# All attention of a two-block transformer kernel taken in pairs of score tiles, with transposes in place of diagonal products

## The chip, the cores and the metric

The kernel runs on one core of one Trainium2 chip. Its engines are called here PE (TensorE, matrix products), DVE (VectorE), ACT (ScalarE), POOL (GpSimd) and SP (SyncE, which issues most of the transfers). The metric is the time of one execution on the device in microseconds (us), lower is better; the median of several executions is given. All data are fp32, and every product with a weight is made from a high and a low part of both operands (three products of the fp32r type in place of one), so PE has three times the work of a plain product. The products inside the attention are plain fp32 products; in the trace each of them is two PE records ("passes").

## The reference, cut to what matters

Two blocks run one after the other on 256 tokens of width 1024. The first one has a layer with retention and a layer with neighbourhood attention ("nat", 16 heads of width 64, 256 image tokens against 256 image keys and 256 context keys), the second one has two layers with three attention branches each.

```python
# nat_mixer: s_nb are scores with a bias by position, s_cx those against the context
p = jax.nn.softmax(jnp.concatenate([s_nb.reshape(B, H, GRID_W, nk), s_cx], axis=-1), axis=-1)
o = einsum(p_nb, vw) + einsum(p[..., nk:], vc)
# _diff_attention, 4 heads, two score tiles each
w = probs(q1, k1) - lam * probs(q2, k2)
o = jnp.einsum('bhqk,bkhd->bqhd', w, v)
# _moba_attention (4 heads of 128; one block of 256 keys, so plain causal attention with a bias)
# _dense_causal_attention, "mla" (8 heads, q and k of width 96, v of width 64)
p = jax.nn.softmax(jnp.where(rel >= 0, s, NEG_INF_2), axis=-1)
o = jnp.einsum('bhqk,bkhd->bqhd', p, v)
```

## The kernel before, in words

Each engine has its own program, written in the same order of stages, and they meet by semaphores. A weight product is a `gemm`: groups of 256 weight columns, a group being two or four chunks (a chunk fills one of the four PSUM banks `bank`), each chunk 24 passes of PE for a depth of 1024. The weights of a group arrive by DMA in `raw`; ACT makes `w_high` and DVE `w_low` of them one or two groups ahead. A chunk is taken out of PSUM by ACT and DVE in turn.

Attention is cut into tiles of 128 queries of one head, and a tile into units: one unit is one softmax (nat, moba and mla have one unit in a tile, diff two, of which the second is multiplied by minus lambda). There are 32 nat units of 512 keys, and in each of the two layers of the second block 16 diff units, 8 moba units and 16 mla units, half of 128 keys and half of 256. One unit goes this way:

- PE `scores`: the product of q and k into `aux[0]` or `aux[1]` (L1948) and the bias added by a second product with a constant matrix (L1949). For nat and diff the product has 64 rows, heads lying at partitions 0 to 63 or 64 to 127.
- DVE `row_max`: the largest score of a row (L1455), and its sign turned (L1456).
- ACT `exponentials`: exp with the row sum beside it (L1016).
- DVE `diagonal`: the reciprocal of the sum (L1465) and the identity times it, a diagonal matrix `dg` (L1468, L1471 with lambda).
- PE `turn`: the probabilities times the diagonal, per 128 keys (L1965), which transposes and divides them in one product, into `aux[2]`; the two units of a diff tile are summed here.
- ACT `turn_out`: `aux[2]` copied to SBUF (L997).
- PE `values`: the turned probabilities with v, per 128 keys, into `aux[3]` (L1979). For nat and mla the result fills 64 partitions, `128*64` in the trace.
- ACT `out_high` (L1005) and DVE `out_low` (L1480): high and low part of the result. There is one bank `aux[3]`, so `values` of a tile waits for `out_low` of the tile before.

The generator `attention` on each engine yields after each unit, and `alongside` puts groups of other weight products between the units: for nat in four calls (nat0 to nat3) of eight units, beside the three products q, k and v of the next four heads, one whole group after units 3, 6 and 8, and none beside nat3; for diff and mla by a rule on the number of units (`narrow`), with DVE and ACT one group behind PE; moba runs bare but for its first units. Four heads' bias tables for nat are fetched by POOL into `tt`, which holds two heads, and DVE adds a mask to them with six instructions a head (L1491).

Of the kernel before, what the change touches and what calls it, by code (L numbers as in the profile page):

```python
# [14 lines left out]
F32 = mybir.dt.float32  # L15
F32R = mybir.dt.float32r
I32 = mybir.dt.int32
ALU = mybir.AluOpType
# [3 lines left out]
P = 128  # L22
# [84 lines left out]
def program(nc, A):  # L107
    ctx = ExitStack()
    with ctx:
# [44 lines left out]
        def scope(tensors):  # L154
            with ExitStack() as s:
# [18 lines left out]
        att_bufs = [("pexp", [P, 2, 512], F32), ("ptr", [P, 2, 512], F32), ("dg", [P, 2, P], F32),  # L174
                    ("stat", [P, 4, 8], F32)]
        ptr = hf
        nah, nal, nq, nk, nv, tt, pexp, dg, stat = scope(first_named(first[:5], "n_") + [
            ("nat_high", [P, DC, T], F32R), ("nat_low", [P, DC, T], F32R), ("nq", [P, DC, T], F32),
            ("nk", [P, DC, T2], F32), ("nv", [P, 4, D], F32), ("tt", [P, 2, 6, 64], F32), att_bufs[0]] + att_bufs[2:])[5:]
        (yh, yl, yt, sq2, hf2, ah, al, sig, v2, v3, mq, mk, mv, t5, ang, oraw,  # L180
         pexp2, dg2, stat2) = scope([
# [5 lines left out]
             ("oraw", [P, 4, T], F32), ("pexp2", [P, 4, T], F32), ("dg2", [P, 4, P], F32),  # L187
             ("stat2", [P, 4, 8], F32)])
        ptr2 = hf2
# [269 lines left out]
        unit_total = tile_total = 0  # L459

        def add_att(name, tiles, bufs):
            nonlocal unit_total, tile_total
            a = Att()
            a.name, a.tiles, a.bufs = name, tiles, bufs
            a.u0, a.t0 = unit_total, tile_total
            a.units = [(t, i) for t, tile in enumerate(tiles) for i in range(len(tile["units"]))]
            unit_total += len(a.units)
            tile_total += len(tiles)
            a.u1, a.t1 = unit_total, tile_total
            a.narrow = name[:3] != "nat"  # L470
            a.slots = 4 if a.narrow else 2
            a.lead = 2 if a.narrow else 1
            atts[name] = a

        tiles = []
        for hd in range(NH):
            c, r = hd // 2, 64 * (hd % 2)
            for qt in range(2):
                tiles.append(dict(
                    units=[dict(qk=(nq[r:r + 64, c, P * qt:P * qt + P], nk[r:r + 64, c, :]), coef=None,  # L480
                                bias=(0, T, tt[:, hd % 2, 2 - 2 * qt:6 - 2 * qt, :]))],
                    keys=512, rows=(r, r + 64),
                    v=lambda k, hd=hd: nv[:, k, 64 * hd:64 * hd + 64],
                    out=(nah[r:r + 64, c, P * qt:P * qt + P], nal[r:r + 64, c, P * qt:P * qt + P]),
                    head=hd))
# [1786 lines left out]
```

## Time and profile before

| | |
|---|---|
| Median of 3 runs | 3334.35 us (3333.47 to 3337.49) |
| The profiled execution | 3335.01 us |
| Its span in the trace | 3333.2 us |
| PE busy | 3189.2 us, 96% of the span |
| PE weight loads busy | 2758.7 us, 83% |
| DVE busy | 1838.9 us, 55% |
| ACT busy | 1167.0 us, 35% |
| Mean granted PE clock | 0.976 of full |

The execution is about 1.8 us longer than the span, which is what lies around the traced program. The busy time of an engine is the union of its records. A record of PE reaches from the start of a pass to the modelled end of it, about 0.17 us after the next may begin, so that what a pass costs is read from the start of one to the start of the next, not from its duration. "Idle <- X" names what released the engine; "issue" stands where the profile found no releaser.

### The profile page before, as it was taken

Reading aid. Unit: us, or ns where it says so; the run is one execution under the profiler, and the core shown is the slowest. Engines: PE = TensorE matmul, PEld = TensorE weight load, DVE = VectorE, ACT = ScalarE, POOL = GpSimd, SP = SyncE. Lnnn points to the kernel's source line nnn. Section 1 sums busy time; section 2 is a strip of 40 time slices with the busy share of each in tenths; the row PEclk is TensorE's granted clock in tenths of the full one; section 3 lists DMA queues with packets and bytes.
Section 4 is the critical chain, followed back from the end, with each engine's and each line's share of the span. In section 5 each row is a group of like instructions: output and inputs, shape, how many; then the busy total and the mean of one; then the engine's idle time right before and its main releaser. Section 6 shows DMA issues by size and latency. Waiting matters only on the chain. (4 is left out here: it accounts for less than half of the span.)

```text
span 3333.2 us, 47025 instructions
## 1 busy us (share of the span) xinstructions
PE 3189.2 (96%) x19173; PEld 2758.7 (83%) x19173; DVE 1838.9 (55%) x3647; ACT 1167.0 (35%) x2007; POOL 62.3 (2%) x106
## 2 busy tenths in 40 slices
PE   7999999999989999999998999999989999999898
PEld 4788887888868888788887777999878999788898
DVE  1677654444458876533324434556556655655665
ACT  2322223233232222332223324444444444344443
POOL 1000000000000000000000000000001000001000
PEclk9999999999989999899998999999999999999999
DMA  8445542212226565433323222655225454324452
GB/s 263 114 137 170 150 161 64 66 61 83 70 64 180 191 191 176 133 90 106 94 82 94 63 63 69 195 168 187 77 89 177 152 183 133 114 89 140 139 189 90
DMA packets 501214, 421.36 MB, mean 126 GB/s; under 512 B 9946, under 2 KB 497674, under 8 KB 501000
## 3 DMA queue, kind: packets, MB, share of 16 engines
q1 hardware_dynamic: 497976, 412.33, 40.3%
q0 software_dynamic: 3024, 6.03, 0.7%
q8 instruction: 152, 2.49, 0.3%
q14 instruction: 62, 0.51, 0.0%
HBM read 417.20 MB, written 1.12 MB: 126 GB/s over the span
## 5 line engine op out<-in xcount | busy, mean ns | idle before, releaser
L1254 DVE TENSOR_TENSOR w_low<-raw,w_high 128x1024 fp32r<-128x1024 f32 (+2 forms) x720 | 761.9, 1100 | 358.5 <-ACT w_high L839 357.4
L839 ACT ACTIVATE w_high<-raw 128x1024 fp32r<-128x1024 f32 (+2 forms) x720 | 647.8, 948 | 689.3 <-PE gemm L1872 408.9
L1872 PE MATMUL gemm<-xh,w_high 128*128 128x512 f32 (+1 forms) x1792 | 675.9, 377 | 22.3 <-DVE xl L1290 22.3
L1872 PE MATMUL gemm<-xl,w_high 128*128 128x512 f32 (+1 forms) x1792 | 666.3, 372 | 0.0
L1872 PE MATMUL gemm<-xh,w_low 128*128 128x512 f32 (+1 forms) x1792 | 666.0, 372 | 0.0
L1872 PEld LDWEIGHTS gemm<-xh,w_high 128*128 128x128 f32 x1792 | 341.2, 190 | 94.2 <-issue 18.3
L1872 PEld LDWEIGHTS gemm<-xh,w_low 128*128 128x128 f32 x1792 | 341.3, 190 | 63.2
L1872 PEld LDWEIGHTS gemm<-xl,w_high 128*128 128x128 f32 x1792 | 341.9, 191 | 60.7 <-issue 0.7
L1872 PE MATMUL gemm<-yh,w_high 128*128 128x256 f32 x1216 | 353.6, 291 | 15.4 <-DVE yl L1315 7.1
L1872 PE MATMUL gemm<-yl,w_high 128*128 128x256 f32 x1216 | 348.1, 286 | 0.0
L1872 PE MATMUL gemm<-yh,w_low 128*128 128x256 f32 x1216 | 347.7, 286 | 0.0
L1225 DVE SCALAR_TENSOR_TENSOR macc<-raw,sc,macc 128x256 f32<-128x256 f32 x728 | 302.1, 481 | 4.0
L1872 PE MATMUL gemm<-hid_high,w_high 128*128 128x512 f32 (+1 forms) x704 | 262.3, 373 | 0.0
L1872 PE MATMUL gemm<-act_high,w_high 128*128 128x256 f32 (+1 forms) x880 | 251.1, 285 | 8.6 <-DVE yt L1422 8.6
L1872 PE MATMUL gemm<-hid_high,w_low 128*128 128x512 f32 (+1 forms) x704 | 259.3, 368 | 0.0
L1872 PE MATMUL gemm<-hid_low,w_high 128*128 128x512 f32 (+1 forms) x704 | 259.2, 368 | 0.0
L1872 PEld LDWEIGHTS gemm<-yh,w_high 128*128 128x128 f32 x1216 | 235.5, 194 | 20.6 <-issue 17.4
L1872 PE MATMUL gemm<-act_low,w_high 128*128 128x256 f32 (+1 forms) x880 | 248.5, 282 | 0.0
L1872 PE MATMUL gemm<-act_high,w_low 128*128 128x256 f32 (+1 forms) x880 | 248.3, 282 | 0.0
L1872 PEld LDWEIGHTS gemm<-yl,w_high 128*128 128x128 f32 x1216 | 235.9, 194 | 0.1
L1872 PEld LDWEIGHTS gemm<-yh,w_low 128*128 128x128 f32 x1216 | 235.4, 194 | 0.0
L1398 DVE TENSOR_TENSOR hf<-sq,gemm 128x512 f32<-128x512 f32 (+1 forms) x88 | 54.6, 621 | 283.5 <-PE gemm L1872 283.5
(307 smaller groups left out, 4429.2 us busy)
## 6 DMA issues: line engine op xcount, KB each, us to landing
raw<-in_ffn_w_in SPq DMA_DIRECT2D x176, 512.0 KB, 5.2
raw<-in_w_mod SPq DMA_DIRECT2D x72, 1024.0 KB, 7.0
raw<-in_w_in SPq DMA_DIRECT2D x50, 1024.0 KB, 5.3
raw<-in_w_up SPq DMA_DIRECT2D x32, 1024.0 KB, 5.5
raw<-in_w_down SPq DMA_DIRECT2D x32, 1024.0 KB, 5.2
raw<-in_ffn_w_out SPq DMA_DIRECT2D x32, 768.0 KB, 4.5
raw<-in_ret_w_in SPq DMA_DIRECT2D x24, 1024.0 KB, 5.2
raw<-in_ffn_w_out SPq DMA_DIRECT2D x32, 640.0 KB, 4.1
```

The costliest lines, as they stand in the source:

```text
L839: act.activation(wh[i % SPL][:, a:b], raw[slot_of["w", i]][:, a:b], ACT.Copy).then_inc(w_high, 1)
L1225: dve.scalar_tensor_tensor(out=acc, in0=raw[slot][:, WB * k:WB * k + WB], scalar=sc[:, k, v:v + 1], in1=acc, op0=ALU.mult, op1=ALU.add).th ...
L1254: dve.tensor_tensor(wl[slot][:, a:b], raw[slot][:, a:b], wh[i % SPL][:, a:b].bitcast(F32), ALU.subtract).then_inc(w_low, 1)
L1398: dve.tensor_tensor(hf[:, pr % 2, 0:tok], sa[:, pr % 2, 0:tok], ps[:, 0:tok], ALU.mult).then_inc(odd_free, 1)
L1872: ins = pe.matmul(out, l_, r_, start=first and j == 0, stop=last and j == 2)
```

## The change

Units are now taken in pairs. For nat and mla a pair is two neighbouring heads with the same 128 queries, for moba two heads, for diff the two softmaxes of one tile. For a pair:

- `scores` makes the two products with 64 rows one directly behind the other (nat and diff: into `aux[0]` and `aux[1]`), then the two biases. For moba and mla both units share a bank, and two pairs can be open at once; for nat and diff the next pair's products wait until both exponentials are out.
- `row_max` has the sign in the same instruction (`negate=True`), and for moba and mla one instruction serves both units.
- `divide` takes the place of `diagonal`: one reciprocal for both sums, and the probabilities themselves are multiplied in SBUF (for diff scaled and added, so that one tile is left).
- `turn` is a transpose on PE (`pe.transpose`) of the divided probabilities, four for each of the 32 nat units, and 24 for each of diff, moba and mla over both layers (48 for mla).
- `values` writes the two heads of a nat or mla pair alternately into the lower and upper 64 partitions of `aux[3]`, and `out_high` and `out_low` take both at once.
- There is one nat attention of 16 pairs, and the nine products nat_q1 to nat_v3 run beside it by single chunks (24 chunks, one after nearly every half pair), until three pairs before its end.
- `tt` holds four heads, and the mask is one instruction a head.

The core of the diff:

```diff
+                def divide(p):
+                    g, t = a.p0 + p, a.pairs[p]
+                    dve.wait_ge(p_ready, 2 * g + 2)
+                    chain(dve.reciprocal(stat_of(a, p, 2), stat_of(a, p, 1)))
+                    first_, second = probs_of(a, p, 0), probs_of(a, p, 1)
+                    if a.kind == "dif":
+                        co = t["layer"]
+                        chain(dve.tensor_scalar(second, second, stat_of(a, p, 2, 1), lamn[:, co:co + 1], ALU.mult, ALU.mult))
+                        dve.scalar_tensor_tensor(out=first_, in0=first_, scalar=stat_of(a, p, 2, 0), in1=second,
+                                                 op0=ALU.mult, op1=ALU.add).then_inc(p_scaled, 2)
+                    else:
+                        dve.tensor_scalar(first_, first_, stat_of(a, p, 2, 0), None, ALU.mult).then_inc(p_scaled, 1)
+                        dve.tensor_scalar(second, second, stat_of(a, p, 2, 1), None, ALU.mult).then_inc(p_scaled, 1)
...
-                        for kt in range(tile["keys"] // P):
-                            for q in range(nu):
-                                uq = u - nu + 1 + q
-                                ins = pe.matmul(aux[2][:, P * kt:P * kt + P], pe_[:, uq % a.slots, P * kt:P * kt + P],
-                                                dg_[:, uq % a.slots, :], start=q == 0, stop=q == nu - 1)
+                    if a.nat:
+                        pe.wait_ge(p_scaled, 2 * g + i + 1)
+                        if g or i:
+                            pe.wait_ge(pt_out, 2 * g + i)
+                        for kt in range(4):
+                            ins = pe.transpose(aux[2][:, P * kt:P * kt + P], probs_of(a, p, i)[:, P * kt:P * kt + P], ident)
...
+                scores(0)
                 yield 1
-                for j, (t, i) in enumerate(a.units):
-                    nu = len(a.tiles[t]["units"])
-                    if j + a.lead < n:
-                        scores(j + a.lead)
-                    turn(j)
-                    if i == nu - 1 and t >= 1:
-                        values(t - 1)
+                for p in range(n):
+                    if p + 1 < n:
+                        scores(p + 1)
+                    if p:
+                        values(p - 1)
+                    turn(p, 0)
                     yield 1
-                values(len(a.tiles) - 1)
+                    turn(p, 1)
+                    yield 1
+                values(n - 1)
```

Place one, PE in the nat attention: one unit as the kernel before has it between two others (L1948 is the product, L1949 the bias, L1965 the turn, L1979 the values).

```order
L1948 MATMUL aux<-nk,nq 128x512
L1949 MATMUL aux<-tt,cst 128x256
L1965 MATMUL aux<-dg,pexp 128x128 x4
L1979 MATMUL aux<-hf,nv 64x128 x4
L1872 MATMUL gemm<-xh,w_high 128x256
L1872 MATMUL gemm<-xl,w_high 128x256
L1872 MATMUL gemm<-xh,w_low 128x256
```

The same place of the changed kernel, one half of a pair's round (L1960 the two products, L1964 the two biases, L2013 the values of the pair before, L1985 the transposes of the first unit, then a chunk of a weight product).

```order
L1960 MATMUL aux<-nk,nq 128x512 x2
L1964 MATMUL aux<-tt,cst 128x256 x2
L2013 MATMUL aux<-xt,nv 64x128 x8
L1985 MATMUL aux<-cst,pexp 128x128 x4
L1881 MATMUL gemm<-w_high,xh 128x256
L1881 MATMUL gemm<-w_low,xh 128x256
L1881 MATMUL gemm<-w_high,xl 128x256
```

Two products, two biases and eight values now stand together, and the values come ahead of the turn. The other half of the round is four transposes and a chunk.

Place two, PE in the mla attention of the first layer, kernel before: two units between two groups of weight products.

```order
L1948 MATMUL aux<-mk,mq 128x128
L1949 MATMUL aux<-cst 128x128
L1965 MATMUL aux<-dg,pexp 128x128
L1979 MATMUL aux<-hf,mv 64x128 x2
L1948 MATMUL aux<-mk,mq 128x256
L1949 MATMUL aux<-cst 128x128
L1965 MATMUL aux<-dg,pexp 128x128 x2
L1979 MATMUL aux<-hf,mv 64x128
```

The same place of the changed kernel:

```order
L1960 MATMUL aux<-mk,mq 128x128
L1964 MATMUL aux<-cst 128x128
L1960 MATMUL aux<-mk,mq 128x128
L1964 MATMUL aux<-cst 128x128
L2013 MATMUL aux<-hf,mv 64x128 x2
L1993 MATMUL aux<-cst,pexp 128x128 x4
```

The values stand once for two units, and behind the scores rather than behind the turn.

Place three, DVE at the same place, kernel before: one unit (L1254 and L1417 belong to the weight products).

```order
L1254 TENSOR_TENSOR w_low<-raw,w_high 128x512 x2
L1417 SCALAR_TENSOR_TENSOR h<-diff_qk_gate,gemm 128x256 x2
L1465 RECIPROCAL stat<-stat 128x1
L1468 TENSOR_SCALAR dg<-cst,stat 128x128
L1455 TENSOR_REDUCE stat<-aux 128x1
L1456 TENSOR_SCALAR stat<-stat 128x1
L1480 TENSOR_TENSOR act_low<-aux,act_high 64x128
```

DVE at this place in the changed kernel, one pair:

```order
L1271 TENSOR_TENSOR w_low<-raw,w_high 128x512 x2
L1434 SCALAR_TENSOR_TENSOR h<-diff_qk_gate,gemm 128x256 x2
L1481 RECIPROCAL stat<-stat 128x2
L1489 TENSOR_SCALAR pexp<-pexp,stat 128x256
L1490 TENSOR_SCALAR pexp<-pexp,stat 128x256
L1475 TENSOR_REDUCE stat<-aux 128x2
L1497 TENSOR_TENSOR act_low<-aux,act_high 128x128
```

In both, the low part of a result (L1480, L1497) comes behind the row maximum of a later unit or pair. In the kernel before, the next thing that PE does behind that unit's turn waits for it; in the changed one the values that wait for it come a pair later.

## Rows read from the trace of the kernel before

**Rows 1.** The page: busy us and share; its group of the turns, all attention.
```profile
PE 3189.2 (96%) x19173; PEld 2758.7 (83%) x19173; DVE 1838.9 (55%) x3647; ACT 1167.0 (35%) x2007; POOL 62.3 (2%) x106
...
L1965 PE MATMUL aux<-dg,pexp 128*128 128x128 f32 x496 | 75.1, 284 | 9.7 <-DVE dg L1471 4.2 <-DVE dg L1468 2.5 <-ACT hf L997 2.2
```

**Rows 2.** PE groups of nat, 1818.7:2039.7 us; busy, mean ns, idle before, releaser.
```profile
L1948 PE MATMUL aux<-nk,nq 64*128 64x512 f32 x64 | 36.1, 645 | 3.0 <-ACT pexp L1016 1.6 <-DVE tt L1491 1.4
L1965 PE MATMUL aux<-dg,pexp 128*128 128x128 f32 x256 | 35.3, 282 | 2.3 <-DVE dg L1468 1.9
L1979 PE MATMUL aux<-hf,nv 128*64 128x128 f32 x256 | 34.1, 276 | 10.8 <-issue 10.1 <-DVE nat_low L1480 0.7
```

**Rows 3.** Timeline of one nat unit, start us, us, passes xcount, idle before.
```profile
1952.67 1.12 PE L1948 MATMUL aux<-nk,nq 64*128 64x512 f32 x2
...
1953.72 0.70 PE L1949 MATMUL aux<-tt,cst 128*128 128x256 f32 x2
...
1954.26 1.05 PE L1965 MATMUL aux<-dg,pexp 128*128 128x128 f32 x8
...
1955.26 0.27 DVE L1480 TENSOR_TENSOR nat_low<-aux,nat_high 64x128 fp32r<-64x128 f32 x1
...
1955.63 1.06 PE L1979 MATMUL aux<-hf,nv 128*64 128x128 f32 x8 [0.32 <-issue]
...
1956.62 0.39 PE L1872 MATMUL gemm<-xh,w_high 128*128 128x256 f32 x1
...
1956.84 0.28 PE L1872 MATMUL gemm<-xl,w_high 128*128 128x256 f32 x1
```

**Rows 4.** PE groups of the first mla, 2438.9:2515.3 us, same columns as rows 2.
```profile
L1979 PE MATMUL aux<-hf,mv 128*64 128x128 f32 x48 | 8.3, 282 | 6.9 <-issue 6.9
L1965 PE MATMUL aux<-dg,pexp 128*128 128x128 f32 x48 | 8.2, 280 | 1.0 <-ACT hf L997 0.6 <-DVE dg L1468 0.3
```

**Rows 5.** Timeline of PE in the bare part of the first diff.
```profile
2357.71 0.70 PE L1948 MATMUL aux<-diff_qk_gate 64*128 64x256 f32 x2
...
2361.41 0.49 PE L1948 MATMUL aux<-diff_qk_gate 64*128 64x128 f32 x2
2361.83 0.49 PE L1949 MATMUL aux<-t,cst 128*128 128x128 f32 x2
2362.25 0.48 PE L1948 MATMUL aux<-diff_qk_gate 64*128 64x128 f32 x2
...
2364.61 0.37 PE L1872 MATMUL gemm<-yh,w_high 128*128 128x256 f32 x1
```

**Rows 6.** Timeline of PE in the first moba: its bare part's start and end.
```profile
2417.30 0.38 PE L1948 MATMUL aux<-h 128*128 128x128 f32 x2
2417.52 0.39 PE L1949 MATMUL aux<-t,cst 128*128 128x128 f32 x2
...
2432.38 0.36 PE L1872 MATMUL gemm<-yh,w_high 128*128 128x256 f32 x1
```

**Rows 7.** Timeline: 32 transposes of PE at the start of the program.
```profile
33.13 3.72 PE L2042 MATMUL aux<-cst,xrows 128*128 128x128 f32 x32
```

**Rows 8.** Stretches: us, busy of PE, PEld, DVE, ACT, POOL, granted clock, DMA.
```profile
33.00:36.60 3.60, 3.60 (x33) 3.47 (x32) 0.68 (x1) 2.77 (x6) 0.51 (x1) 1.00 1.10 348
1821.00:1825.00 4.00, 4.00 (x13) 2.55 (x12) 1.83 (x8) 1.79 (x5) 1.29 (x2) 0.57 0.25 82
2417.00:2433.00 16.00, 12.54 (x81) 10.45 (x81) 7.30 (x34) 7.07 (x29) 0.00 (x0) 1.00 0.21 66
```

**Rows 9.** Single lines: ns, min/median/max, over forms of 128, 256 and 512.
```profile
L1455 DVE TENSOR_REDUCE stat<-aux x112: 281/425/693, 1820.5 to 3037.7; 128x1 f32<-128x128 f32 x40, 128x1 f32<-128x256 f32 x40, 128x1 f32<-128x512 f32 x32
L1016 ACT ACTIVATE pexp<-aux,stat x112: 367/473/687, 1821.4 to 3038.3; 128x128 f32<-128x128 f32 x40, 128x256 f32<-128x256 f32 x40, 128x512 f32<-128x512 f32 x32
L1016 ACT ACTIVATION_READ_ACCUMULATOR pexp<-aux,stat x112: 191/193/194, 1822.0 to 3038.7; 128x1 f32 x112
L1219 DVE TENSOR_SCALAR macc<-raw,sc x104: 343/348/360, 103.5 to 1360.1; 128x256 f32<-128x256 f32 x104
```

More of the change, by code:

```diff
@@ L473, in add_att @@
             atts[name] = a
-        tiles = []
-        for hd in range(NH):
-            c, r = hd // 2, 64 * (hd % 2)
+        pairs = []
+        for c in range(NH // 2):
             for qt in range(2):
[L479 to L485, printed above, removed]
@@ L488, in program @@
+        add_att("nat", pairs)
         for l in range(2):
[L489 to L490 removed]
+            pairs = []
             for hd in range(DH):
                 for qt in range(2):
[L493 to L499 removed]
@@ L500, in program @@
-            add_att(f"diff{l}", tiles, B2)
-            tiles = []
-            for hd in range(DH):
+                    n, y0 = P * (qt + 1), P * (1 - qt)
+                    pairs.append(dict(
+                        units=[dict(qk=(q2[r:r + 64, hd, P * qt:P * qt + P], k2[r:r + 64, hd, 0:n]), rows=(0, P), col=0,
+                                    bias=(0, n, t5[:, hd, y0:y0 + n]), v=lambda k, hd=hd: v2[:, k, P * hd:P * hd + P])
+                               for r in (0, 64)],
+                        keys=n, layer=l, ov=aux[3][:, 0:P], out=oraw[:, hd, P * qt:P * qt + P]))
@@ L503, in program @@
+            add_att(f"moba{l}", pairs)
+            pairs = []
+            for c in range(MH // 2):
                 for qt in range(2):
                     n = P * (qt + 1)
-                    y0 = P * (1 - qt)
-                    tiles.append(dict(
-                        units=[dict(qk=(q3[:, hd, P * qt:P * qt + P], k3[:, hd, 0:n]), coef=None,
-                                    bias=(0, n, t5[:, 4 + hd, y0:y0 + n]))],
-                        keys=n, rows=(0, P), v=lambda k, hd=hd: v3[:, k, P * hd:P * hd + P],
-                        out=(ah[:, 4 + hd, P * qt:P * qt + P], al[:, 4 + hd, P * qt:P * qt + P]), head=hd))
@@ L523, in program @@
-            add_att(f"mla{l}", tiles, B2)
+                    pairs.append(dict(
+                        units=[dict(qk=(mq[0:96, 2 * c + i, P * qt:P * qt + P], mk[0:96, 2 * c + i, 0:n]),
+                                    rows=(64 * i, 64 * i + 64), col=0,
+                                    bias=(P * qt, P * qt + P, cst[:, C_CAUSAL:C_CAUSAL + P]),
+                                    v=lambda k, c=c, i=i: mv[:, k, P * c + 64 * i:P * c + 64 * i + 64]) for i in range(2)],
+                        keys=n, ov=aux[3][:, 0:P],
+                        out=(ah[:, 8 + c, P * qt:P * qt + P], al[:, 8 + c, P * qt:P * qt + P])))
@@ L1187, in _ @@
                 run(gate)
[L1188 removed]
+                alongside(f"mla{l}", attention(f"mla{l}"), both(*(gemm(o) for o in with_mla(l))), 1)
                 for q in range(4):
@@ L2218, in _ @@
                 pe.wait_ge(sub_t, DH * (l + 1))
-                for x in range(len(atts[f"moba{l}"].units)):
+                for x in range(2 * len(atts[f"moba{l}"].pairs)):
                     next(steps)
```

434 lines of the change are left out of this document (217 added, 217 removed).

## The prediction

> **What bounds the kernel now.** I read the page first: PE is busy 96% of the span, DVE 55% and ACT 35% [rows 1], so a microsecond taken from PE's own row of work is a microsecond of the whole, wherever no other wait comes up behind it. So the second view is PE's groups in the stretch of each attention: in nat three groups of attention work at 34 to 36 us busy each, and 16 us of idle time beside them [rows 2]. The third is the timeline, which gives the price of each piece from start to start.
>
> One nat unit runs from 1952.67 to 1956.62, 3.95 us [rows 3]: product 1.05, bias 0.54, turn 0.98 (8 passes) with 0.32 idle behind it (some units show 0.45), values 0.99. The idle time is put down to "issue", but the row of DVE says what it is: the low part of the result before ends at 1955.53, and PE's values start 0.10 later [rows 3]. It is late because it stands behind the row maximum of the scores just made. So: 32 units at 4.0 are 128 us. Four separate attentions also start cold, about 2 us each for the three later ones (waits before values, a turn and scores at each start, 6 us of the 16 in [rows 2]). Together 134 us of attention in the stretch, the rest are weight products.
>
> **Prices on PE.** A full-height product of 128 columns takes 0.22 us for its two passes (2417.30 to 2417.52) [rows 6], a 64-row one of the same width 0.42, and the bias behind it 0.42 again [rows 5]. So going into the 64-row shape and out of it costs 0.20 each time. A pass of 128 columns is 0.11, and 0.98 for 8 passes plus 0.13 for the change to 64 columns fits the values [rows 3]. 32 transposes take 3.72 us, less the modelled tail of 0.2 that is 0.11 each, one pass and not two [rows 7].
>
> **Nat, -28.** A pair in the changed kernel: two products 2 x 0.86 and one exit 0.19, two biases 1.08, 16 passes of values 1.72 and two changes of shape 0.26, eight transposes 0.9 and 0.2 of starts: 6.1 us, where two units were 8.0. 16 pairs are 98. I add 8: about 2 at the start, where the second pair's products wait for both exponentials of the first with nothing to cover it; 2 for 15 more returns to a weight product, whose first pass takes 0.22 rather than 0.12 [rows 3]; 0.7 at the one half pair with no chunk behind it; 3 for the last three pairs and the tail, which run bare. 134 - 106 = 28. The wait for the low part goes: values now wait for the low part of two rounds earlier. What is late next in the covered part: from the scores of a pair to its first transpose go two row maxima (0.69 each), two exponentials (0.69 and 0.19 for the read-out of the sum, the second behind a copy that I take as 0.6), the reciprocal and the division of 512, for which the nearest row is 0.35 for 256 on DVE, by which I take 0.48: some 4.6 us [rows 9]. PE has two chunks of at least 24 x 0.12 = 2.9 and the next scores to do in that time, 8 us and more. It is covered. DVE's own load does not grow: 32 x 0.69 as before, two divisions where two diagonals and two sign changes were, about the same time, a mask of one instruction a head where there were six. POOL's fetches of the tables have four slots, and the pair they serve is two pairs away. SP's weights: the stretch gets a seventh shorter, and the DMA engines are 0.25 busy in it [rows 8], so they are hidden.
>
> **Mla, -12 in each layer, -24.** Idle of PE before values and turns is 7.9 us in the first layer [rows 4]; values wait for a low part of a pair earlier now, so I take 7 of it. 48 turn passes (5.2) become 24 transposes (2.7): 2.5. 16 changes to the 64-column shape and back at 0.2 become 8: 1.6. The rest, 0.9, is my allowance for the second start of a pair's values and scores that falls away. Sum 12. One place is worse: the values of the seventh pair stand directly behind its transposes (0.7), I leave it in the rounding. Weight groups still stand between most half pairs and cover the chain.
>
> **Diff, -5 in each layer, -10.** A head takes 6.9 us now (2357.71 to 2364.61, bare) [rows 5], 6.6 over eight units, 28 us in a layer. PE's own work for it falls to about 4.6, but the chain is bare and single-buffered here: from a pair's first product to the next pair's, with 256 keys, 1.9 for products, exit and biases, 0.2 until the data stand, the second maximum 0.42 partly behind the first, two exponentials at 0.47 + 0.19: 3.6. With 128 keys 2.6. That is 6.2 a head, 25 in a layer, less what the two groups of weight products cover, 2 us: 23. PE's transposes and values fit in the gaps. The scaling and adding of two tiles on DVE (0.35 by [rows 9], and I take 0.5 for the one with two inputs) lies beside the next scores. Bounds: 0, if DVE's row maximum gets stuck behind that division each time, and -9, PE's own work.
>
> **Moba, -2.4 in each layer, -5.** The bare part is 15.1 us now (2417.30 to 2432.38) [rows 6]. Chaining the four pairs (scores 0.9 or 1.75, one maximum of 0.42 or 0.69, two exponentials, two divisions of 0.3, transposes, copy, values) I get 12.7. PE waits for ACT's copy and DVE's division in it, as now.
>
> **An unknown: passes beside each other, 0 to -26, taken as -13.** "Products adjacent" puts passes of different halves of the array next to each other, and no row has two such passes in a row. From below: every row shows a pass beginning when the last has had its columns, so 0. From above: if a pass in one half may begin beside the last one in the other, the order is a0 b0 a1 b1, b0 and a1 run together, four slots become three: 0.43 x 16 for nat, 0.3 x 8 for diff; the values' 16 passes become 9 slots, 0.75 x 16 for nat, and 0.5 x 8 for mla. Sum 26. The 0.20 at each change of shape [rows 5] says that the array is really set up differently for them, which a mere zero padding would not need, so I don't take 0; since the two passes of one product and the weight loads in between may still hold it up, I don't take all. Half, 13.
> The Trainium skill, "TensorEngine Tiling (Array Packing)", section Key Properties, says that tiles work independently and may load and multiply in parallel; by that rule alone the time would be that of the second case below.
>
> **Sum.** 28 + 24 + 10 + 5 + 13 = 80 us. 3335.0 - 80 = 3255 for an execution like the profiled one, which is 0.7 above the median of the runs: 3254 predicted.
>
> **Rivals.**
> - *Full overlap.* The sum with 26 rather than 13: 3241. For it: the shape changes cost time, so the shapes exist. Against: no row shows two passes at once.
> - *Chains bind.* Without overlap, diff and moba give nothing, and in nat each of 26 half pairs waits 0.5 for DVE or ACT, which also split weights and empty banks in between: 28 - 13 + 24 = 39, 3295. For it: the order now ties two units to one semaphore. Against: the 8 us of cover worked out above. Half of it gives 3280.
> - *Clock.* PE had 0.57 of its clock, so the lower level of 1.2 GHz nearly throughout, in 1821 to 1825, behind 1.4 us of waiting and 64-row products; it had 1.00 (2.4 GHz) in the bare part of moba, busy 78% [rows 8]. The bare pairs will leave PE busy some 75%. If they ran at the lower level, their 25 us a layer would grow by about half of PE's share in the chain, 8 us, and the weight group behind them would lose 3: +25 in all with nat's end, 3280. Against: transposes alone ran at 1.00 in 33.0 to 36.6 [rows 8]. The skill's page "TensorE: Matmul & The Clock Gate", Part 4, holds that transposes do not count as activity in the same way, which speaks for this rival; those 3.6 us do not bear it out, though they follow other work.
> - *Slower.* ACT takes exponentials, the copies of turned tiles, results and half the banks in one strict order, and the first copy of a pair now stands between its two exponentials, waiting for PE. If that closes a loop over a chunk (PE's scores of the next pair wait for the second exponential, which waits for the copy, which waits for a turn behind a chunk), each of 16 nat and 16 diff pairs pays a chunk. It decides from 67 / 32 = 2.1 us a pair; at 3 us it is 3335 + 96 - 67 = 3364. By the order the turn stands ahead of the chunk, not behind it, so I give it little.
>
> **Chances.** Forecast with a half overlap, 3247 to 3268: 0.55. Full overlap, 3241 and a little under: 0.18. Chains bind in part, about 3280: 0.12. Clock, 3280: 0.08. No change within 0.2% (7 us, about what a measurement of this kernel can tell): 0.03. Slower: 0.04. The range reaches over the full overlap, with some us for waits that I left in, and up to the bound of the chains: 3228 to 3292. Faster 0.93, same 0.03, slower 0.04.
>
> **What the profile of the changed kernel would show.** Nat stretch: 190 us or less where there were 221, PE's "issue" idle before values gone; a nat pair's own PE work 6.1 without and 5.0 with overlap, seen by values of 16 passes taking 1.8 or 1.0 from start to the next. The turns' group falls from 75 us busy [rows 1] to about 25. Mla from 76 to 64 us between its first product and its last group. Diff a period of 6 us a head, with PE idle on the exponentials. Clock 1.00 in the bare parts. Wrong would be: chunks waiting for banks in nat, PE idle before the transposes for `p_scaled` by more than 0.3 each, or a clock under 0.9 in these stretches.

## The result and the profile after

The changed kernel takes 3228.57 us (median of four runs, 3227.58 to 3230.89) where the kernel before takes 3334.98 (3333.47 to 3337.49): the ratio is 0.968, with a 95% interval of 0.966 to 0.970. That is 106 us less; 80 were forecast, and the time lies inside the forecast range by only 0.6 us (its lower end was 3228). The profiled execution took 3227.6 us with a span of 3225.8, 107.4 under the span of before, so the two traces can be compared directly.

The page of the changed kernel, busy time and share, answers to [rows 1]:

```profile
PE 3094.3 (96%) x18901; PEld 2696.4 (84%) x18901; DVE 1801.9 (56%) x3335; ACT 1152.2 (36%) x1943; POOL 62.2 (2%) x106
```

PE is still the bound, at the same share of a shorter span. Measured from the first product of a stage to the step behind its last values, the two traces give:

| stage | before | after | difference | forecast without overlap |
|---|---|---|---|---|
| nat | 221.0 | 160.4 | -60.5 | -28 |
| diff, layers 1 and 2 | 45.7, 45.7 | 40.3, 38.5 | -5.5, -7.2 | -5 each |
| moba, layers 1 and 2 | 22.1, 22.1 | 19.3, 20.4 | -2.8, -1.6 | -2.4 each |
| mla, layers 1 and 2 | 76.4, 76.4 | 62.8, 62.8 | -13.6, -13.6 | -12 each |

Together 104.8; the rest lies between the stages. More than half of the gain, and most of what the forecast lacks, is in nat.

One pair in nat, in the timeline of PE (start, us, passes xcount; the weight products between are left out). In nat the probabilities lie in `pexp` and `sq` by turns, and the turned tiles in `hf` and `xt`:

```profile
1857.53 1.13 PE L1960 MATMUL aux<-nk,nq 64*128 64x512 f32 x4
1858.59 1.13 PE L1964 MATMUL aux<-tt,cst 128*128 128x256 f32 x4
1859.65 1.09 PE L2013 MATMUL aux<-hf,nv 128*64 128x128 f32 x16
1860.68 0.66 PE L1985 MATMUL aux<-cst,sq 128*128 128x128 f32 x4
...
1861.09 0.37 PE L1881 MATMUL gemm<-w_high,xh 128*128 128x256 f32 x1
...
1863.98 0.60 PE L1985 MATMUL aux<-cst,sq 128*128 128x128 f32 x4
...
1864.34 0.36 PE L1881 MATMUL gemm<-w_high,xh 128*128 128x256 f32 x1
```

From start to start: four passes of the products take 1.06 us, and in [rows 3] the two passes of one unit took 1.05. Sixteen passes of values take 1.03, where eight took 0.99. The biases take 1.06, the transposes 0.41 and 0.36. Together 3.92 us of PE's own work for a pair. The same timeline cut to 1857.50:1857.56 still shows two passes of the product:

```profile
1857.53 0.70 PE L1960 MATMUL aux<-nk,nq 64*128 64x512 f32 x2
```

Two passes of 0.53 us have begun within 0.03 us of each other. The two halves of the array work at the same time, in full.

What PE waits for in nat now (groups of 1819.6:1980.2, the columns of [rows 2]):

```profile
L1964 PE MATMUL aux<-tt,cst 128*128 128x256 f32 x64 | 18.1, 405 | 0.0
L1960 PE MATMUL aux<-nk,nq 64*128 64x512 f32 x64 | 18.1, 640 | 4.5 <-DVE tt L1506 2.6 <-ACT pexp L1013 1.8
L1985 PE MATMUL aux<-cst,sq 128*128 128x128 f32 x64 | 10.1, 280 | 1.7 <-ACT xt L1023 1.7
L1985 PE MATMUL aux<-cst,pexp 128*128 128x128 f32 x64 | 10.0, 279 | 1.7 <-ACT hf L1023 1.7
L2013 PE MATMUL aux<-hf,nv 128*64 128x128 f32 x128 | 8.8, 279 | 0.7 <-ACT hf L1023 0.7
```

The 10.1 us of "issue" before values in [rows 2] are gone. In their place stand waits for ACT's copies, most of them in the bare pairs at the end, and a second one for the mask (1.11, beside the 1.5 that opens nat). The product's group has halved, 36.1 to 18.1 us, and values went from 34.1 to twice 8.8, with the same number of passes.

In the first mla (2370.0:2432.9, answering to [rows 4]) the 6.9 us of "issue" before values are gone; values now wait 1.5 for ACT's copy, and one wait for the division has come up:

```profile
L1993 PE MATMUL aux<-cst,pexp 128*128 128x128 f32 x24 | 4.1, 279 | 1.2 <-DVE pexp L1490 1.2
L2013 PE MATMUL aux<-turned,mv 128*64 128x128 f32 x32 | 2.6, 285 | 0.0
L2013 PE MATMUL aux<-hf,mv 128*64 128x128 f32 x16 | 1.8, 298 | 1.5 <-ACT hf L1027 1.5
```

The bare part of the first moba, in PE's timeline (to [rows 6]): from 2351.59 to 2364.32, 12.7 us, with its largest wait in between.

```profile
2351.59 0.59 PE L1960 MATMUL aux<-h 128*128 128x256 f32 x2
...
2361.31 0.68 PE L2013 MATMUL aux<-hf,v 128*128 128x128 f32 x4 [1.58 <-DVE act_low L1497]
...
2364.32 0.37 PE L1881 MATMUL gemm<-yh,w_high 128*128 128x256 f32 x1
```

### The profile page after: what moved, and what is told of

It reads as the page before. It is cut to its first block and busy times, and to the rows that moved or that the text cites. A ratio compares the mean times of both kernels' runs of the same rounds, so it can differ in the third digit from the quotient of the medians.

```text
span 3225.8 us, 45812 instructions
## 1 busy us (share of the span) xinstructions
PE 3094.3 (96%) x18901; PEld 2696.4 (84%) x18901; DVE 1801.9 (56%) x3335; ACT 1152.2 (36%) x1943; POOL 62.2 (2%) x106
```

## The experiments

Each run is compared with the changed kernel (3228.57 us), but for the one that edits the kernel before.

**Products not adjacent.**

```diff
-                    if a.apart:
-                        product(0)
-                        product(1)
-                        with_bias(0)
-                        with_bias(1)
-                    else:
-                        for i in range(2):
-                            product(i)
-                            with_bias(i)
+                    for i in range(2):
+                        product(i)
+                        with_bias(i)
```

> The changed kernel with one thing undone: in nat and diff each unit's bias follows its own product, so the two 64-row products of a pair no longer stand next to each other. Overlap theory (two adjacent 64-row products run side by side in full, as their 4 passes take 1.06 us from start to start in the changed kernel, where one unit's 2 took 1.05): a nat pair loses 1.05 us, 16 x 1.05 = 17, and a diff pair at most 0.2 to 0.6, since its chain is bare and the first maximum now starts earlier, so 1 to 5 in all: 3228.6 + 18 to 22 = 3247 to 3251. Rival (no overlap; the passes are short for another reason and adjacency saves only one exit from the 64-row shape and one entry, 0.4 together): 16 x 0.4 = 6, 3235, with two passes of 512 at about 0.5 in both orders.

Measured: 3274.87 us (3272.74 to 3276.60), 46 more than the changed kernel and more than twice what was expected. The timeline of a covered pair has what the overlap theory says, per unit 1.05 for the product and 0.63 for the bias:

```profile
1857.42 1.12 PE L1960 MATMUL aux<-nk,nq 64*128 64x512 f32 x2
1858.47 0.70 PE L1964 MATMUL aux<-tt,cst 128*128 128x256 f32 x2
1859.10 1.09 PE L2007 MATMUL aux<-xt,nv 128*64 128x128 f32 x16
```

That is 2 x 1.68 in place of 2.12, 1.25 a pair and 20 in nat. But nat is 32.4 us longer, and diff 4.3 in the first layer and 13.1 in the second (some 5 us come back elsewhere). Part of the rest is in the stretches (us, busy of PE, PEld, DVE, ACT, POOL, granted clock, DMA), first of this kernel:

```profile
1821.00:1833.00 12.00, 10.40 (x19) 4.24 (x19) 3.64 (x7) 2.54 (x7) 0.80 (x2) 0.50 0.05 15
...
1986.00:2000.00 14.00, 13.16 (x39) 6.03 (x38) 3.42 (x7) 3.70 (x9) 0.00 (x0) 0.54 0.19 51
2841.00:2857.00 16.00, 15.95 (x69) 12.75 (x70) 7.16 (x17) 5.12 (x15) 0.00 (x0) 0.59 0.00 0
```

and of the changed kernel, at the start and the end of nat:

```profile
1821.00:1833.00 12.00, 10.17 (x72) 8.36 (x71) 6.48 (x11) 6.04 (x13) 2.58 (x4) 1.00 0.33 85
1963.00:1980.00 17.00, 12.22 (x104) 7.92 (x104) 6.78 (x18) 7.73 (x19) 0.00 (x0) 1.00 0.22 61
```

At the start of nat the granted clock is 0.50 (1.2 GHz) in the one and 1.00 (2.4 GHz) in the other. Both open nat with the same wait of 1.5 us. Behind it the one ran four 64-row products one by one, each with its bias, and the clock was back at 1.00 with the first weight products; the other ran them two at once. The kernel with all three undone, further down, has the same order there and the same 0.50. It is not the shape of the product alone, though: the kernel before with its low part first, also further down, has single 64-row products at this place too, with turns between them, and was granted 1.00 in 1821 to 1833:

```profile
1821.00:1833.00 12.00, 11.38 (x64) 7.89 (x65) 6.22 (x22) 5.86 (x13) 2.59 (x4) 1.00 0.25 71
```

So adjacency is worth its passes and, in bare stretches of this kernel, also some of the clock: the mean granted clock was 0.967 or 0.968 in all four executions without it, and 0.974 or 0.975 in the four of the changed kernel. Why the clock falls there is not shown.

**Not adjacent in covered pairs alone.** The condition becomes `a.apart and not (a.nat and 2 <= p <= 11)`.

> The first experiment narrowed: the products are not adjacent in ten of nat's sixteen pairs only, the third to the twelfth, all with weight products between their halves; the other pairs and diff keep them adjacent. With everything undone the kernel took 46 us more, and its trace shows two things: in each covered pair 1.25 us more of PE's own work (two units of 1.05 and 0.63 where four passes take 1.06 and four biases 1.06), and the granted clock at 0.5 to 0.85 behind the bare pairs of nat and in diff's second layer. Theory: the first is the price of the passes, the second a price of bare stretches. Then here 10 x 1.25 = 12.5, 3241, and the clock stays at 1.00 in 1820 to 1960. Rival (64-row products one by one pull the clock down wherever they stand): 3250 or more, with low clock in the covered pairs.

Measured: 3241.18 us (3240.79 to 3243.07), 12.6 more than the changed kernel where 12.5 were expected, and the stretch of covered pairs at full clock:

```profile
1840.00:1940.00 100.00, 99.16 (x642) 74.54 (x641) 42.36 (x77) 37.87 (x78) 10.33 (x16) 1.00 0.25 73
```

That settles the first term of the 46 us (those of the first experiment): a non-adjacent pair costs 1.25 us and does not touch the clock between weight products. So 20 us are passes in nat, and the 12 that nat lost beyond them are put down to its clock at both edges. The rest is diff: its second layer, at 0.59 for 16 us, lost 13.1, and its first 4.3.

**Values one unit after the other.**

```diff
-                    if a.kind in ("nat", "mla"):
-                        seq_ = [(i, kt) for kt in range(nkt) for i in range(2)]
```

> The changed kernel with one thing undone: the passes of values in nat and mla run through one unit of the pair and then through the other, where they alternated between the two 64-column halves. Overlap theory (alternating products run side by side): nat's 16 passes go from 1.03 us to twice 0.99, + 0.95 x 16 = 15; mla's 8 passes from 0.59 to about 1.0 and its 4 passes from 0.37 to about 0.55, + 0.3 x 8 in each layer, 5 in both: 3228.6 + 20 = 3249, or some 3 less where a stall in mla takes it up. Rival (the order among the passes is of no account, what is saved is only the second start and the shape changes): 3229 to 3231.

Measured: 3235.37 us (3233.73 to 3236.34), 6.8 more, a third of what was expected; nat is 7.8 longer, mla not at all. The sixteen passes take 1.51 us from start to start (1859.87 to 1861.38), not 1.95:

```profile
1859.87 1.58 PE L2011 MATMUL aux<-hf,nv 128*64 128x128 f32 x16
1861.38 0.66 PE L1985 MATMUL aux<-cst,sq 128*128 128x128 f32 x4
```

Cut to its first 0.43 us (1859.86:1860.29), the timeline shows four passes begun; the changed kernel's, cut alike (1859.64:1860.07), eight:

```profile
1859.87 0.65 PE L2011 MATMUL aux<-hf,nv 128*64 128x128 f32 x4
```

```profile
1859.65 0.66 PE L2013 MATMUL aux<-hf,nv 128*64 128x128 f32 x8
```

So four passes run alone, and all sixteen fit into twelve slots of 0.11: 12 x 0.11 + 0.2 for the changes is 1.51, 8 slots would be 1.03 and 16 would be 1.95. The second unit starts beside the fifth pass of the first, with three passes of the first unit still to come. In mla a unit has two or four passes, no more than that lead, and 8 passes take 0.59 or 0.60 us in either order. PE takes passes of the free half ahead of their turn, with three or four passes of the other half still to come; this is read from the counts and not from the records' names, which don't tell the units apart. Both theories of this run were wrong: the order matters, but only beyond that lead.
The Trainium skill, "TensorE: Matmul & The Clock Gate", Part 3, says that matmuls start and end strictly in program order; these counts speak against it for the start, and the measurement decides.

**Turns by a product with the identity.** `pe.transpose(out, probs, ident)` becomes `pe.matmul(out, probs, ident, start=True, stop=True)`.

> The changed kernel with one thing undone: each turned tile is a plain product with the identity instead of a transpose. I expect two passes in place of one: four in a row 0.88 to 1.0 us where four transposes take 0.36 to 0.41. Nat: 32 fours, + 0.55 x 32 = 18. Mla: 24 tiles in a layer, + 0.12 x 24 = 3 in each; moba 12 tiles, + 1.4 in each, diff 12, + 1 in each, bare. Sum 18 + 11 = 29, less what stalls take up: 3228.6 + 22 to 29 = 3251 to 3258. Rival (PE waits for the chain behind the turns anyway, so the passes' number counts only in part): half of it, 3243.

Measured: 3247.41 us (3242.24 to 3250.01), 18.8 more. Four turns take eight passes and 0.91 or 0.81 us, in place of 0.41 and 0.36: 32 x 0.47 = 15, and nat is 15.0 longer. In mla 2.2 of the expected 3 a layer came. In diff and moba the difference looks like next to nothing (from -1.0 to +1.0 a stage), but part of that is the clock: the changed kernel lost some of it in its first diff and its second moba (0.96 in both, the lines below), and this run was granted 1.00 in all four stages. The two stages that ran at 1.00 in both are 0.5 longer (the second diff, 38.5 to 39.1) and 1.0 longer (the first moba, 19.3 to 20.3), where 1 and 1.4 were expected. So the passes count in full in nat, and by a half to three quarters in the other stages, where stalls take up the rest.

```profile
2284.00:2325.00 41.00, 35.45 (x251) 30.67 (x250) 20.29 (x51) 14.57 (x53) 0.00 (x0) 0.96 0.26 78
...
2851.00:2872.00 21.00, 17.24 (x124) 15.89 (x122) 9.00 (x27) 7.82 (x27) 0.00 (x0) 0.96 0.25 76
```

**All three undone.**

> All three undone together: products not adjacent, values one unit after the other, turned tiles by plain products with the identity; the pairs, the new order of work, the division ahead of the turn and the chunks between stay. If the three pay on different pieces of PE's row and none covers the other, the rises add: 20 + 20 + 26 = 66, 3295, and pairing and order by themselves are worth the remaining 40 of 106. Rival (they share one slack, chains that come up once PE's passes are short): the sum is over or under the parts by more than 8 us.

Measured: 3290.55 us (3286.68 to 3293.67), 62 more than the changed kernel; the three one by one sum to 72. Nat is 48.0 longer here and 55.2 by the sum. This kernel's clock fell at the start of nat and in the first diff, but not at the end of nat, where that of the first experiment stood at 0.54 for 14 us. Seven of the 10 us between lie in nat, so they are mainly a clock that fell at an edge in one execution and not in the other. What is left for pairs and the new order by themselves is 44 us; no run divides it further. The second diff ran at full clock here: 43.4 us, which is 4.3 more than with the turns alone undone (39.1). That is what adjacency is worth in one layer of diff without the clock.

**Chunks by whole groups.** In nat, `gemm(..., by_chunk=True)` loses its argument and the steps are nine: `upto = min(9, (3 * x + 7) // 8)`.

> The changed kernel with one thing undone: in nat the weight products of the next heads come by whole groups (some 9 pieces of 5.8 to 11.6 us) between half pairs, no longer by single chunks (24 pieces of 2.9). The same work, another place. Each pair's chain from scores to turn to copy is then bare in about 15 more of the 32 halves. Theory: a bare half waits 0.6 to 0.8 us (0.84 and 0.75 for ACT's copies behind the last pairs), so + 9 to 12, 3238 to 3241, and the clock may fall behind bare pairs, + 3 more. Rival (what is between the halves matters little, as one chunk of 2.9 us covers two halves): + 0 to 3, 3229 to 3232.

Measured: 3235.37 us (3233.62 to 3235.84), 6.8 more, between the two. PE's groups of nat show five waits of 0.84 for each of ACT's two copies, where there were two:

```profile
L1985 PE MATMUL aux<-cst,sq 128*128 128x128 f32 x64 | 10.2, 282 | 4.2 <-ACT xt L1023 4.2
L1985 PE MATMUL aux<-cst,pexp 128*128 128x128 f32 x64 | 10.1, 281 | 4.2 <-ACT hf L1023 4.2
```

The price of a bare half was right (six more, 5.0 us, and 1.2 more for the mask), their number was not: six wait that did not, and not 15.

**The kernel before, with the low part first.**

```diff
-                    if j + a.lead < n:
-                        row_max(j + a.lead)
                     if j and a.units[j - 1][0] != t and t >= 2:
                         out_low(t - 2)
+                    if j + a.lead < n:
+                        row_max(j + a.lead)
```

> The kernel before with one line moved: DVE takes the low part of a result ahead of the row maximum of the next scores, not behind it. The prediction read PE's idle time before values (0.32 to 0.45 us a unit in nat, 6.9 us in a layer of mla, all put down to issue) as waiting for that low part, standing behind the maximum. If that is so, it goes where the low part can be ready: nat about 20 units at 0.35 = 7, mla some 4 to 6.9 in each layer, less what the later maximum gives back: 3334 - 13 = 3321, between 3313 and 3327. Rival (the values wait for ACT's copy of the turned tile, and the low part is not what comes last): 3334, within 3.

Measured: 3313.45 us (3312.39 to 3314.82), ratio 0.994 (0.992 to 0.995): 21.4 us less than the kernel before, by two statements that change places. The groups of PE before values, first in nat, then in the first mla, where [rows 2] and [rows 4] had 10.1 and 6.9 us of "issue":

```profile
L1979 PE MATMUL aux<-hf,nv 128*64 128x128 f32 x256 | 34.7, 278 | 3.4 <-issue 2.7 <-DVE nat_low L1480 0.7
```

```profile
L1979 PE MATMUL aux<-hf,mv 128*64 128x128 f32 x48 | 8.6, 288 | 0.0
```

So that idle time was the wait for the low part behind the row maximum. Nat is 7.7 us shorter, mla 5.1 and 5.2, diff and moba 0.4 and 0.9 a layer. That is as much as a fifth of the change's gain, from an order alone.

**Diff with single chunks.** `with_diff(l)` comes by chunks, one behind each of the first seven pairs: `upto = min(nb - 1, 1 + x // 2) + (x == na)`.

> The changed kernel with the weight products beside diff cut into single chunks of 24 passes (2.9 us), one behind the turn of each of the first seven pairs and one at the end, where there were two groups of 48 within and two behind it. The bare pairs of diff show PE idle for 5.6 us in the first layer (1.03, 0.60, 0.59, 0.58, 0.61 for the exponentials, the rest for the division and the last copy) and then 1.4 us of lower clock. Theory: a chunk of 2.9 covers the way from scores to the second exponential, so 4 to 5 us go in each layer and the clock stays at 1.00: 3228.6 - 9 = 3219.5. Rival (ACT and DVE also empty the chunks' banks in between, in strict order, so that the exponentials come later by as much): 3226 to 3229.

Measured: 3234.76 us (3233.53 to 3238.69), 6 us more instead of 9 less. From the first product of diff to the first of moba it takes 63.2 us in both layers, where the changed kernel took 60.9 and 59.1. (Its profiled execution was the slowest of the four; the clock also stood at 0.50 for 13 us at the end of nat, which this edit does not touch.) All engines, in one place of the first diff:

```profile
2297.61 1.22 DVE L1273 TENSOR_TENSOR w_low<-raw,w_high 128x1024 fp32r<-128x1024 f32 x1
...
2298.74 0.42 DVE L1386 SCALAR_TENSOR_TENSOR h<-gemm,rstd 128x256 f32<-128x256 f32 x1
2299.08 0.15 DVE L1483 RECIPROCAL stat<-stat 128x2 f32<-128x2 f32 x1
2299.27 0.41 DVE L1487 TENSOR_SCALAR pexp<-pexp,stat,lam_negated 128x256 f32<-128x256 f32 x1
2299.80 0.48 DVE L1488 SCALAR_TENSOR_TENSOR pexp<-pexp,stat 128x256 f32<-128x256 f32 x1
...
2300.34 0.44 PE L1995 MATMUL aux<-cst,pexp 128*128 128x128 f32 x2 [1.97 <-DVE pexp L1488]
```

With the chunk, DVE splits the next block of weights and empties a bank before it divides, and PE's turn waits 1.97, 1.59 and 1.39 us for the division where it waited 0.16 and 0.36. The wait for the exponentials is gone, as expected, but the clock did not stay at 1.00 (0.57 in 2301 to 2305 and in 2332 to 2336); what took its place is the second theory's strict order, on DVE. A second set of score banks for diff, which would take that wait away in another way, was not tried: its two products write two banks at once, and turns and values hold the other two.

**The maximum ahead of the division in moba and mla.** In DVE's loop `row_max(p + 1)` stands before `divide(p)` unless `a.apart`.

> The changed kernel with DVE's row maximum of the next pair ahead of the division of this pair in moba and mla, whose scores have two banks, so that the next scores are already there. After the change PE waits there 3.4 us in each bare part of moba (1.07, 1.58, 0.77) and 4.5 us in each mla (1.21 for the division, 0.73 for a bank, 1.47 for a copy, 1.12). Theory: the next exponentials start one division (0.6 to 0.8 us) earlier in each pair, and half of the waits go: 3228.6 - 4 = 3224.5. Rival: the turn of this pair waits for that division and gets it one maximum (0.42 to 0.69) later, so the wait only moves: 3228 to 3231.

Measured: 3236.84 us (3235.79 to 3238.39), 8 us more. In mla, the wait for the division is 4.2 us where it was 1.2, and each mla is 3.3 us longer (66.1):

```profile
L1995 PE MATMUL aux<-cst,pexp 128*128 128x128 f32 x24 | 4.2, 282 | 4.2 <-DVE pexp L1490 4.2
```

The rival holds, and is worse than written: the wait doesn't only move.

**And the result written early.** On top of it, ACT's `out_high(p - 1)` stands before `exponentials(p + 1, 0)` in moba and mla.

> The same, and in moba and mla ACT also writes the result of the pair before ahead of the next pair's exponentials, not behind both, so that DVE's low part of it and PE's next values (which wait 1.58 us for that low part in moba) come earlier. Moving DVE's low part took 21 us off the kernel before, 5 of them in each layer of mla. Theory: - 1.5 in moba and - 1 in mla beyond the last, in each layer: 3219.5. Rival: ACT now waits for PE's values before it takes the exponentials, which stand 0.4 to 0.9 us behind the scores, and passes that on: 3224 to 3230.

Measured: 3236.55 us (3235.72 to 3239.33), the same as the last; mla 65.8, moba 20.4. The rival holds, though not by its number (3224 to 3230): in the bare part of moba one wait of 0.81 for the low part became one of 0.67 for ACT's copy. In this profile the clock also stood at 0.54 at the end of nat, in instructions which no edit touches:

```profile
1973.00:1985.00 12.00, 8.97 (x55) 7.45 (x55) 2.44 (x6) 5.73 (x9) 0.00 (x0) 0.54 0.00 0
```

**Nat's edges.** `upto = min(nb, x + 1 - (x + 6) // 13)`, and `mask_bias(p + 3)`, `mask_bias(p + 4)` in the odd pairs, ahead of the chunk.

> The changed kernel with two edits to nat's edges: the first chunk of weight products stands ahead of the second pair's scores (where PE waits 1.83 us for the first exponentials), with one chunk less towards the end, and DVE adds the mask to a pair of bias tables one half pair earlier, since it stood behind a chunk's bank and PE waited 1.11 us for it. Theory: - 1.83 + 0.84 - 1.11 = - 2, 3226.5. Rival: the weights for that first chunk are not split yet, so the wait is the same under another name, and the bare end gets one pair longer: 3228 to 3230.

Measured: 3228.51 us (3226.07 to 3231.42), no difference that can be told. In its trace nat takes 158.5 us, 2.0 less, and the waits for the exponentials and the second one for the mask are gone, with one of 0.9 for the division in their place:

```profile
L1960 PE MATMUL aux<-nk,nq 64*128 64x512 f32 x64 | 18.1, 641 | 1.5 <-DVE tt L1506 1.5
```

Two microseconds in one trace are less than the runs of one kernel differ by, so whether they are kept stays open. Its four executions lie apart with their mean clock: 3226.07 and 3226.78 at 0.975 and 0.974, 3230.25 and 3231.42 at 0.972.

**A try at the best of both.** The edges of nat, and in moba and mla division, low part, maximum in this order on DVE, with ACT's result first.

> A try at a version that beats both: the two edits to nat's edges, which took 2.0 us off the stretch of nat in its trace (160.4 to 158.5), and in moba and mla the division first, then the low part of the pair before, then the row maximum of the next pair on DVE, with ACT writing that pair's result ahead of the next exponentials. The runs with the maximum ahead of the division lost 3.3 us in each layer of mla, since the turn waited for the division. Theory: with the division back in front that loss is gone, and the low part ahead of the maximum takes off what it took off the kernel before, a part of the 1.58 us in moba and of the bank waits: 3228.6 - 2 - 2 = 3224.5. Rival: DVE now waits for PE's values and ACT's write before it takes the maximum, so the next exponentials come 0.5 us later in each bare pair: moba and mla + 1 to 2 a layer, 3229 in all.

Measured: 3240.36 us (3235.38 to 3244.48), 12 us more. Moba is 22.5 in both layers (19.3 and 20.4), mla 64.6 and 66.1. Some of this is the clock: the five executions have a mean of 0.970 to 0.974, and the one at 0.974 took 3235.38, 7 us more than the changed kernel at about that clock. In the profiled one, which was the slowest, it stood at half at the end of nat and at the end of the first moba's bare part:

```profile
1972.00:1986.00 14.00, 11.34 (x65) 9.83 (x66) 3.59 (x6) 5.45 (x9) 0.00 (x0) 0.52 0.00 0
2365.00:2372.00 7.00, 5.07 (x22) 4.67 (x23) 1.63 (x5) 2.97 (x10) 0.00 (x0) 0.51 0.01 2
```

In this bare part one wait for ACT's copy is 2.64 us:

```profile
2366.17 1.22 PE L2017 MATMUL aux<-hf,v 128*128 128x128 f32 x4 [2.64 <-ACT hf L1027]
```

The second moba, at full clock until its last 4 us, shows the same wait of 2.64. So the rival holds, and the loss is a mixture of its price and the clock. Its account, that DVE waits for PE's values and ACT's write before the maximum, so that the next exponentials and the copy behind them come later, fits these waits. The low part ahead of the maximum by itself, which gained 21 us in the kernel before, was not run in the changed kernel, so this does not show that it loses there. No version was found that beats the changed kernel.

## Why the prediction came out as it did

- **What bounds the kernel.** Right. PE kept its 96%, and the reading of "issue" as the wait for the low part [rows 3] is shown by the kernel before with its low part first.
- **Prices on PE.** Those of single 64-row and full passes hold. Four transposes take 0.41 and 0.36 from start to start, less than the 0.55 priced for four with their start.
- **Nat, -28 and a share of the overlap; measured -60.5.** The waits are 8.5 us in the trace (1.83, 1.11, four of 0.84, two of 0.75, and 0.70), where some 6 of the 8 allowed were waits. What was mis-sized is a pair's own work, 3.92 us and not 6.1: products 1.06 for 1.91, values 1.03 for 1.98, transposes with their start 0.77 for 1.1. 16 x 2.2 = 35, against a difference of 32.5. The term that was mis-sized is thus the overlap of the next point, with the transposes as a small second (5 us of the 35).
- **The overlap, 0 to -26, taken as -13: the step that failed.** Its upper bound held the passes to their order: a0 b0 a1 b1, "four slots become three". In the trace four slots are two and sixteen are eight, as both halves start together. On the prediction's own terms that is 0.85 x 16 + 0.95 x 16 = 29 in nat where the bound had 19. The reading that led to it, that a change of shape costs time and so the shapes are real, pointed the right way. The rule named there (the Trainium skill, "TensorEngine Tiling (Array Packing)", Key Properties: tiles work independently and may load and multiply in parallel) holds in this trace in full, two passes within 0.03 us. The upper bound of 26 was worked out by me and was no bound; its own terms, 6.9 + 2.4 + 12 + 4, add to 25.
- **Full overlap** was a rival at 3241, given 0.18, and is the case that came, 12 us lower: nat had 10 more of overlap than the bound allowed and 5 more from the transposes. That the time still fell inside the range, by 0.6 us, is luck: it reached that low for waits that might not come, not for more overlap.
- **Mla, -12 a layer.** Measured -13.6, but the terms are others. Of 7.8 us of waits 3.4 are left (1.2 for the division, 0.7 for a bank, 1.5 for ACT's copy), so 4.4 went where 7 were forecast. The other 9.2 is PE's own work, where 5 were forecast without overlap: 8 passes of values take 0.59 in this kernel. The two misses cancel.
- **Diff, -5 a layer.** Measured -5.5 and -7.2, the first with some 1.6 lost to the clock (the same stage took 38.7 in the run with covered pairs not adjacent, at 1.00). The 5 were forecast without overlap, and that is not where they came from: adjacency is worth 4.3 in either layer at like clock (44.6 for 40.3, 43.4 for 39.1), and without it the first diff is only 1.2 less than before. The chain of a bare pair starts with its scores, and most of the gain is that these are shorter. That was a miss, hidden by the other.
- **Moba, -2.4 a layer.** Measured -2.8 and -1.6. The bare part was chained by hand to 12.7 us and takes 12.7, in part by luck: the largest wait in it is 1.58 for the low part, where waits for the copy and the division were told, and none is for the division. The second layer lost 1.1 to the clock (granted 0.66 in 2870 to 2875).
- **Chains bind.** Not in nat's covered part. In bare pairs they do, as told.
- **Clock.** It fell for a moment in the changed kernel, 0.66 in 2317 to 2322 behind the bare part of diff, some 1.6 us there, and 0.66 in 2870 to 2875, where the prediction had 1.00 in the bare parts and named a clock under 0.9 as a sign of being wrong. The rival had the places right. Its reason, that bare pairs leave PE idle for a quarter of the time, is not enough: the bare part of moba, busy 8.59 of 12 us, ran at 1.00. Once adjacency is gone it costs some 20 us (12 in nat, 9 in the second diff). That adjacent products go with a higher clock, the prediction did not see.
- **Slower.** ACT's order never closed the loop that was feared; the wait for its copies is 0.8 in bare halves.

## What to carry to other kernels

Where two products of half height or half width use different halves of the array, put their passes next to each other: they cost the time of one. Here products of half height wrote two banks, and products of half width the two halves of one bank; no run tried two products of half height in one bank. Look at every idle time before the bounding engine put down to "issue" and find the other engine's instruction that ends 0.1 us ahead of it; the order of two statements on an engine busy 55% was worth 21 us in the kernel before. Before an edit is judged by a few microseconds, compare the granted clock of the same stretches in both traces, since two stages here seemed to gain nothing and had only lost it elsewhere. And when a wait is cured by moving work to it, name what the other engines do for that work first, since DVE split weights and emptied a bank ahead of the division that PE needed.

## What the runs showed of the hardware

- Two 64-row passes of 512 columns in fp32 begin together and take 0.53 us from start to start, as one did; so do two 64-column passes of 128, at 0.11.
- A pass of the free half is begun ahead of its turn, with three or four passes of the other half still to come: 16 passes in 1.51 us with eight of one half ahead of eight of the other, and no loss with four ahead of four (0.60 and 0.59).
- In 1821 to 1833, the bare start of nat, the granted clock was 0.50 in the two kernels that ran four 64-row products one by one, and 1.00 in the changed kernel, which ran them two by two. With single products and turns between them it was 0.86 in the kernel before and 1.00 in the same kernel with its low part first; and in one run with adjacent products (the maximum ahead of the division) it was 0.86. So what makes it fall is not shown.
- At the bare end of nat it stood at 1.00 in the changed kernel's profile and at 0.54 in another for the same instructions. At which of these edges it falls differs from one execution to the next, and that is worth some us of a comparison.
- A turn by transposing is one pass, by product with the identity two: 0.41 and 0.91 us for four.
